# Expert layers: a gathered slot holds 32 tokens by four experts, and two slots are multiplied together in four sets of 32 columns

## The chip, the cores and the metric

One core of a Trainium2 chip runs the whole program. The metric is the device time of one execution in microseconds (us).

The engines are TensorE (PE in the profile; its weight loads are PEld), VectorE (DVE), ScalarE (ACT), GpSimd (POOL) and SyncE (SP). They run side by side, each through its own list in order, and wait for one another on semaphores. POOL issues the indirect transfers (gathers); SP issues the plain ones.

## The reference: what is computed

A decoder trunk of two layers for 512 prompt tokens and 8 sample tokens, all in float32, model width 1024. Layer 0 mixes tokens by a gated delta rule, layer 1 by latent attention with a paged cache. After each mixer comes the channel mixer, called PEER here, which is what the change is about:

```python
def peer_ffn(xn, w_q, sub_keys, u_tab, v_tab):
    q = (x2 @ w_q).reshape(T, PEER_HEADS, 2, PEER_HALF)
    s = jnp.einsum('thpd,hpnd->thpn', q, sub_keys)        # 2 x 128 keys per head
    ...                                                    # top 16 of each, then top 16 of the 256 sums
    h = jnp.einsum('td,ted->te', xb, u_tab[ib])            # per token, 8 heads x 16 experts
    act = jax.nn.gelu(h, approximate=False) * gb
    return jnp.einsum('te,ted->td', act, v_tab[ib])
```

So each token takes 128 expert rows out of a table of 16384, each row a u vector and a v vector of 1024 floats (8 KB together), a dot product with the token, a GELU and a gate, and the weighted sum of the v vectors. Each token has its own experts, so the rows are gathered one by one.

## The kernel before, in words

`peer` (L1429) runs once per layer. The prompt's 512 tokens are four tiles of 128. A **unit** is one head of one tile: 128 tokens by 16 experts, `UNITS` = 32 per layer. Units 0 to 15 take tiles 0 and 1 in turn, units 16 to 31 tiles 2 and 3 (`tile_of`, L1498). A unit is 16 **slots**; a slot is one gather of 128 rows of 8 KB (1.05 MB) into one of the 8 places of `ring` (L1455). So a layer has 512 slots, plus 8 for the sample tokens at its end. Before the change a slot holds 64 tokens by two experts: partition p of slot c holds an expert of token p mod 64.

The way of one slot, c of unit u:

- **POOL** (L1566) waits until the slot's place is free, which is the semaphore `pv` of the slot 8 places earlier, and issues the gather.
- **DVE** (L1761) waits for the landing and multiplies the u half by `rep`, the normed tokens repeated for the two experts, summing into one column of `hs`.
- **ACT** makes the GELU (L1642), multiplies by the gate (L1646) and writes the slot's entry of `diag` (L1650), a 128x64 matrix with the weights on two diagonals.
- **PE** (L1951) multiplies `diag` by the v half in two matmuls, one per half of the 1024 columns: each has 64 array columns and 512 moving columns, and they go to two halves of the partitions of a PSUM bank `acc`. Eight slots add up into one bank, and DVE adds the bank to `x` (`add`, L1721). The second matmul raises `pv` by one.

Between these, and in the same lists, stands the selection for the next unit: PE makes scores after the `pv` of slot 0 (`score`, L1895), DVE finds the top 16 in two parts after slots 1 and 4 (`retrieve`, L1705), PE spreads the 16 columns of indices over the two halves of the partitions after slot 5 (`lay`, L1905), DVE writes them as `idx` at slot 7 (`place`, L1710), and the same is done for the gates at slots 8 to 12. PE also projects the queries of the next head (L1883).

`rep` for a tile is made by `repeat` (PE, L1887) and `repeated` (ACT, L1606): a matmul with a constant that picks 64 tokens and writes them twice over the partitions, then a copy out of PSUM. It is done 4 times per tile: 2 groups of 64 tokens by 2 halves of the width. One PSUM bank (`pq`) serves, so each matmul waits for the copy before it. For tile 0 this is ahead of the first unit, between the scores and `lay` on PE; for tiles 1 and 3 in slots 0 to 3 of units 0 and 16; for tile 2 in slots 2 to 5 of unit 15.

Part of the latent attention is also run in these lists as a background (`Causal`, called as `back` at every slot number n from `BACK[layer]`, L1424): in layer 0 from unit 16 on, in layer 1 from unit 0 to about unit 14. It has transfers of its own on SP, and steps on PE, ACT and DVE with due slots.

Of the kernel before, what the change touches and what calls it, by code (L numbers as in the profile page):

```python
# [30 lines left out]
P = 128  # L31
D = 1024
# [29 lines left out]
N_CONST = C_REP + 2  # L62
HALF = D // 2
TG = 64
GS = SEQ // TG
# [770 lines left out]
class TopK:  # L836


    def __init__(self, core, ctx, n):
# [6 lines left out]
        self.crest = sb(ctx, "crest", [n, TOPK, TOPK])  # L846
# [77 lines left out]
class Causal:  # L924
# [369 lines left out]
    def tensor(self, pe, m):  # L1294
        s, core, at, bank = self.s, self.core, self.s.at, self.bank
        if m == 0:
            after(pe, *self.ready["banks"])
        if self.half == 0:
# [130 lines left out]
def peer(core, layer, oT, os, w_out, kept):  # L1429
# [6 lines left out]
    with Marks(core, "peer", **{f"o_w{k}": 16 for k in range(4)}, gain=32, inp=32, w0=32, w1=32, o_made=1, o_added=1, square=1, paired=1, mean=1,  # L1436
               root=1, inverse=1, row=1, turned=1, copied=1, copied2=1, q_first=4, first_out=4, q_made=2, q_out=2, scored=1, top=TOP_STEPS,
               exped=1, gate=2, mixed=2, placed=1, gated=1, rep_made=4, rep_out=4, dot=TOPK, gelu=TOPK, factor=TOPK, diag=TOPK, pv=TOPK, added=2,
# [15 lines left out]
        rep = core.sbuf(ctx, "rep", [P, 4, D])  # L1454
# [9 lines left out]
        diag = core.sbuf(ctx, "diag", [P, RING, TG])  # L1464
# [5 lines left out]
        spread = core.sbuf(ctx, "spread", [H * NS, 2, H, TOPK])  # L1470
# [3 lines left out]
        sac = core.sbuf(ctx, "sac", [P, NS, TG])  # L1474
# [13 lines left out]
            "xn": (at("rep_made", 3 - 2 * layer, 4),),  # L1488
            "x": (at("added", HEADS - 1, 2),),
            "banks": ((s["o_added"], done), (s["copied"], (done + 1) // 2), (s["copied2"], done // 2), (s["mean"], done), (s["first_out"], 4))})  # L1490
# [7 lines left out]
        def tile_of(u):  # L1498
            return 2 * (u // HEADS) + u % 2

# [22 lines left out]
        with nc.Block() as block:  # L1523
# [54 lines left out]
            def _(act):  # L1578
# [27 lines left out]
                def repeated(t, i):  # L1606
# [3 lines left out]
                    act.activation(rep[:, 2 * (t % 2) + i // 2, column(i % 2)], pq[:, :], ACT.Copy).then_inc(s["rep_out"], 1)  # L1610
# [16 lines left out]
                for i in range(4):  # L1627
                    repeated(0, i)
# [8 lines left out]
                for u in range(UNITS):  # L1637
                    a, hh = u % 2, u // 2 + 1
                    for c in range(TOPK):
# [10 lines left out]
                        act.activation(diag[:, c % RING, :], core.const[:, C_PAIR, 0:TG], ACT.Copy, scale=hgg[a][:, c:c + 1]).then_inc(s["diag"], 1)  # L1650
# [6 lines left out]
                        if u in (0, HEADS) and c < 4:  # L1657
                            repeated(tile_of(u + 1), c)
                        if u == HEADS - 1 and 2 <= c < 6:
                            repeated(2, c - 2)  # L1660
# [19 lines left out]
            def _(dve):  # L1680
# [12 lines left out]
                def row(g):  # L1693
                    after(dve, (s["inverse"], g + 1))
                    if 4 <= g < GS:
                        after(dve, at("rep_made", (g - 4) // 2, 4))
# [33 lines left out]
                dve.memset(sac[:, :, :], 0.0).then_inc(s["szero"], 1)  # L1730
# [21 lines left out]
                for u in range(UNITS):  # L1752
                    a = u % 2
                    for c in range(TOPK):
                        n = TOPK * u + c
                        if c == 0:
                            after(dve, at("rep_out", tile_of(u), 4))
# [3 lines left out]
                        dve.scalar_tensor_tensor(ring[:, c % RING, 0:D], ring[:, c % RING, 0:D], 1.0, rep[:, 2 * a + c // RING, :],  # L1761
# [26 lines left out]
                        if u == UNITS - 1:  # L1788
# [989 lines left out]
```

## Time and profile before

| | us |
|---|---|
| median of 3 runs | 3997.41 |
| lowest and highest | 3995.16, 4000.92 |
| span of the profiled execution, first to last instruction | 3986.4 |
| PE busy | 3005.8 |
| DVE busy | 2474.6 |
| ACT busy | 1535.0 |
| POOL busy | 1289.7 |

The trace is of one execution. No time of that execution from outside is given beside its span; the median stands 11.0 us above the span. In the span the gathers of layer 0 run from 695 to about 2120 us and those of layer 1 from 2515 to about 3965 us. A row that groups instructions gives the count, the busy time (overlaps counted once), the mean time of one in ns, then the idle time ahead of them and what ended it. A float32 matmul stands as two instructions, since it is done in two passes. PEclk is the granted clock, 1.00 being the full one.

### The profile page before, as it was taken

How to read it: one execution, taken by the hardware profiler on the slowest of the kernel's cores; microseconds unless marked ns; L12 is line 12 of the kernel's file. 1: busy time of each engine (PE TensorE's matmuls, PEld its weight loads, DVE VectorE, ACT ScalarE, POOL GpSimd, SP SyncE). 2: the span in 40 equal slices, each digit the busy share in tenths (PEclk: the TensorE clock that was granted, in tenths of full speed). 3: DMA queues.
4: the chain of work that ended last, by engine and by line, in shares of the span. 5: the costliest groups of instructions: out<-in, count | busy, mean ns of one | idle time of the engine just before them, and what ended most of it. 6: DMA issues, size and time to landing. Idle time of an engine off the chain costs nothing. (4 is left out here: it accounts for less than half of the span.)

```text
span 3986.4 us, 45941 instructions
## 1 busy us (share of the span) xinstructions
PE 3005.8 (75%) x14557; PEld 1439.4 (36%) x14557; DVE 2474.6 (62%) x6084; ACT 1535.0 (39%) x4402; POOL 1289.7 (32%) x1172
## 2 busy tenths in 40 slices
PE   7997888777666677768757798776777876666666
PEld 6886775322212122223313575322232222222221
DVE  2665443676676667767773343476677677667675
ACT  2352121444343344446432221344544444334332
POOL 0004330444434333333441110233334344334433
PEclk9998788988778788888878898888888988787778
DMA  2211002999999999999996453799999999999998
GB/s 89 73 51 55 13 13 71 404 420 416 420 414 418 405 397 387 411 366 384 402 421 244 165 204 144 291 375 390 381 375 415 405 404 421 413 420 413 411 421 334
DMA packets 234350, 1261.33 MB, mean 316 GB/s; under 512 B 32008, under 2 KB 71952, under 8 KB 97552
## 3 DMA queue, kind: packets, MB, share of 16 engines
q0 software_dynamic: 153600, 1133.58, 69.8%
q1 hardware_dynamic: 80528, 125.08, 9.1%
q8 instruction: 105, 1.72, 0.2%
q14 instruction: 117, 0.96, 0.1%
HBM read 1244.25 MB, written 14.19 MB: 316 GB/s over the span
## 5 line engine op out<-in xcount | busy, mean ns | idle before, releaser
L1951 PE MATMUL acc<-ring,diag 128*64 128x512 f32 x4096 | 1339.0, 751 | 751.3 <-ACT diag L1650 748.9
L1569 POOL DMA_INDIRECT ring<-in_uv,idx x1024 | 1119.1, 1093 | 1895.3 <-PE acc L1951 1635.2
L1761 DVE SCALAR_TENSOR_TENSOR ring<-ring,rep 128x1024 f32<-128x1024 f32 x1024 | 1230.6, 1221 | 368.9 <-DMA ring<-in_uv,idx 309.3
L1951 PEld LDWEIGHTS acc<-ring,diag 128*64 128x64 f32 x4096 | 250.3, 158 | 1494.2 <-ACT diag L1650 1317.8
L1642 ACT ACTIVATE hg<-hs 128x1 f32<-128x1 f32 x1024 | 203.7, 199 | 1141.1 <-DVE ring L1761 1139.1
L1650 ACT ACTIVATE diag<-const,hgg 128x64 f32<-128x64 f32 x1024 | 356.4, 348 | 33.4
L1646 ACT ACTIVATE hgg<-hg,weigh_by 128x1 f32<-128x1 f32 x1024 | 302.0, 295 | 33.2
L1883 PE MATMUL big<-xnT,w 128*128 128x264 f32 (+1 forms) x960 | 297.1, 435 | 0.0
L1883 PEld LDWEIGHTS big<-xnT,w 128*128 128x128 f32 x960 | 174.8, 203 | 185.0 <-issue 166.4
L298 PE MATMUL acc<-xnT,w 128*128 128x260 f32 x1024 | 230.2, 386 | 0.7 <-ACT inp L419 0.7
L298 PEld LDWEIGHTS acc<-xnT,w 128*128 128x128 f32 x1024 | 196.3, 192 | 38.4 <-issue 7.5
L1725 DVE TENSOR_TENSOR x<-acc,x 128x512 f32<-128x512 f32 x128 | 88.1, 688 | 117.2 <-PE acc L1951 117.2
L1642 ACT ACT_TABLE_LOAD x102 | 130.9, 1283 | 1.8
L875 DVE MAX8 sv<-mix 128x8 f32<-128x128 f32 x128 | 31.8, 290 | 150.5 <-PE mix L1902 150.3
L561 POOL TENSOR_TENSOR gU<-const,cols 128x512 f32<-128x512 f32 x8 | 8.4, 1045 | 340.8 <-POOLq L135 301.2
L1604 ACT ACTIVATE q<-big 128x264 f32<-128x264 f32 (+1 forms) x60 | 23.3, 388 | 239.5 <-PE big L1883 175.8
L1839 PE MATMUL big<-wo,oT 128*64 128x512 f32 x384 | 96.6, 640 | 19.0 <-DMA wo<-in_w_mla_out 10.8
L2584 DVE COPY cT<-b 128x512 f32<-128x512 f32 x64 | 44.2, 691 | 85.0 <-PE b L2406 84.9
L770 DVE TENSOR_TENSOR U<-pB,U 128x256 f32<-128x256 f32 x48 | 20.4, 425 | 121.6 <-PE pB L626 121.6
L2363 ACT ACTIVATE cT<-b 128x512 f32<-128x512 f32 x64 | 38.1, 596 | 145.1 <-PE b L2406 145.1
L1761 DVE DVE_READ_ACCUMULATOR ring<-ring,rep 128x1 f32 x1024 | 84.9, 83 | 0.0
L1614 ACT ACT_TABLE_LOAD x64 | 82.1, 1283 | 1.1
(571 smaller groups left out, 4057.7 us busy)
## 6 DMA issues: line engine op xcount, KB each, us to landing
w<-in_w_peer SPq DMA_DIRECT2D x64, 512.0 KB
w<-in_w_gdn SPq DMA_DIRECT2D x32, 512.0 KB, 3.6
ring<-in_uv,idx POOLq DMA_INDIRECT x1024, 12.3
wo<-in_w_mla_out SPq DMA_DIRECT2D x8, 1024.0 KB, 11.5
wo<-in_w_uq SPq DMA_DIRECT2D x8, 768.0 KB, 14.2
out_ssm_s<-states SPq DMA_DIRECT2D x4, 1024.0 KB, 5.1
wo<-in_w_gdn_out SPq DMA_DIRECT2D x4, 1024.0 KB, 8.2
sk<-in_keys SPq DMA_DIRECT2D x64, 64.0 KB
```

The lines of the kernel that those rows point to most:

```text
L298: last = pe.matmul(acc[c % 2][:, r, :], w[:, c, k, :], xnT[:, k, PART * r:PART * r + PART], start=k == 0, stop=k == KD - 1)
L1569: pool.indirect_dma_start(out=ring[:, c % RING, :], out_offset=None, in_=uv, in_offset=bass.IndirectOffsetOnAxis(ap=idx[u % 2][:, c:c + 1] ...
L1614: act.activation(k.e[:, :], k.tv[:, :], ACT.Exp, bias=k.low[:, 0:1], accum_out=k.z[:, 0:1]).then_inc(s["exped"], 1)
L1642: act.activation(hg[a][:, c:c + 1], hs[a][:, c:c + 1], ACT.Gelu).then_inc(s["gelu"], 1)
L1646: act.activation(hgg[a][:, c:c + 1], hg[a][:, c:c + 1], ACT.Copy, scale=weigh_by[a][:, c:c + 1]).then_inc(s["factor"], 1)
L1650: act.activation(diag[:, c % RING, :], core.const[:, C_PAIR, 0:TG], ACT.Copy, scale=hgg[a][:, c:c + 1]).then_inc(s["diag"], 1)
L1725: dve.tensor_tensor(core.x[:, g, :], acc[i][:, :], core.x[:, g, :], ALU.add).then_inc(s["added"], 1)
L1761: dve.scalar_tensor_tensor(ring[:, c % RING, 0:D], ring[:, c % RING, 0:D], 1.0, rep[:, 2 * a + c // RING, :], ALU.mult, ALU.mult, accum_ou ...
L1839: last = pe.matmul(summed(g)[rows(j), :], lhs, wo[:, kk, column(j)], start=kk == 0, stop=kk == KD - 1)
L1883: last = pe.matmul(pq[:, 0:n], w[:, p, kk, :], xnT[:, kk, 0:n], start=kk == 0, stop=kk == KD - 1)
L1951: last = pe.matmul(acc[i][rows(j), :], diag[:, r, :], ring[:, r, D + HALF * j:D + HALF * j + HALF], start=r == 0, stop=r == RING - 1)
L2584: dve.tensor_copy(cT[g % 2][:, 1, :, :], b1[g % 2][:, :, :]).then_inc(s["half1"], 1)
```

## The change

A slot now holds 32 tokens by four experts. Two slots, c - 1 and c, are multiplied together: four matmuls (two slots by two halves of the width), each with 32 array columns, each into its own 32 partitions of the bank. `diag` is 32 columns wide. PE waits for the `diag` of the odd slot only, and then raises `pv` twice.

```diff
-C_REP = C_PAIR + 1 ... N_CONST = C_REP + 2
+C_REP = C_PAIR + 1 ... C_QUAD = C_REP + 4; N_CONST = C_QUAD + 1; SUB = 32
-        rep = core.sbuf(ctx, "rep", [P, 4, D])
+        rep = core.sbuf(ctx, "rep", [P, 8, D])
-        diag = core.sbuf(ctx, "diag", [P, RING, TG])
+        diag = core.sbuf(ctx, "diag", [P, RING, SUB])
...
+        def repeat_bank(i):
+            return spare[:, :] if i % 2 else pq
+        def subs(i, b):
+            return slice(TG * i + SUB * b, TG * i + SUB * b + SUB)
...
# ACT
-                    act.activation(rep[:, 2 * (t % 2) + i // 2, column(i % 2)], pq[:, :], ACT.Copy).then_inc(s["rep_out"], 1)
+                    act.activation(rep[:, 4 * (t % 2) + i // 2, column(i % 2)], repeat_bank(i), ACT.Copy).then_inc(s["rep_out"], 1)
-                for i in range(4):
+                for i in range(8):
                     repeated(0, i)
-                        act.activation(diag[:, c % RING, :], core.const[:, C_PAIR, 0:TG], ACT.Copy, scale=...)
+                        act.activation(diag[:, c % RING, :], core.const[:, C_QUAD, 0:SUB], ACT.Copy, scale=...)
                         if u in (0, HEADS) and c < 4:
-                            repeated(tile_of(u + 1), c)
+                            for i in range(2 * c, 2 * c + 2):
+                                repeated(tile_of(u + 1), i)
...
# DVE
-                        ... rep[:, 2 * a + c // RING, :], ...
+                        ... rep[:, 4 * a + 2 * (c // RING) + c % 2, :], ...
-                dve.memset(sac[:, :, :], 0.0)        # ahead of the units
+                            if c == 0:               # in the last unit
+                                dve.memset(sac, 0.0)
...
# PE
 def repeat(t, i):
-                    g = 2 * t + i // 2
-                    after(pe, (s["row"], g + 1), at("rep_out", t, i))
+                    g = 2 * t + i // 4
+                    after(pe, (s["row"], g + 1), at("rep_out", t, i - 1))
...
-                    pe.matmul(pq[:, :], core.const[:, C_REP + i % 2, :], normed(g), ...)
+                    pe.matmul(repeat_bank(i), core.const[:, C_REP + i % 4, :], normed(g), ...)
 def lay(v, e, src):
                     for i in range(2):
-                        for r in range(2):
-                            last = pe.matmul(pR[rows(r), e, RING * i:RING * i + RING], core.const[:, C_ID, rows(i)], src[:, RING * r:RING * r + RING], ...)
+                        for b in range(2):
+                            for r in range(4):
+                                last = pe.matmul(pR[SUB * r:SUB * r + SUB, e, RING * i + b:RING * i + RING:2], core.const[:, C_ID, subs(i, b)], src[:, 4 * r:4 * r + 4], ...)
...
                         n, r, i = TOPK * u + c, c % RING, c // RING
-                        after(pe, at("diag", u, c + 1))
-                        if r == 0:
-                            after(pe, at("added", u - 1, i + 1) if u else (s["o_added"], 4))
-                        for j in range(2):
-                            last = pe.matmul(acc[i][rows(j), :], diag[:, r, :], ring[:, r, D + HALF * j:D + HALF * j + HALF], start=r == 0, stop=r == RING - 1)
-                        last.then_inc(s["pv"], 1)
+                        if c % 2:
+                            after(pe, at("diag", u, c + 1))
+                            if r == 1:
+                                after(pe, at("added", u - 1, i + 1) if u else (s["o_added"], 4))
+                            for b in range(2):
+                                for j in range(2):
+                                    last = pe.matmul(acc[i][subs(j, b), :], diag[:, r - 1 + b, :], ring[:, r - 1 + b, D + HALF * j:D + HALF * j + HALF],
+                                                     start=r == 1, stop=r == RING - 1)
+                                last.then_inc(s["pv"], 1)
...
-    nc = bacc.Bacc("TRN2", target_bir_lowering=False, num_devices=1)
+    nc = bacc.Bacc("TRN2", target_bir_lowering=False, num_devices=1, dynamic_dma_scratch_size=4096)
```

`rep` doubles to 32 KB of each partition, and the room comes from elsewhere: `crest` now lies in `rest`, `spread` and `sac` lie in `rep`, `diag` is half as wide, and the scratch area that the program sets aside for the descriptors of POOL's gathers is set to 4096 bytes per partition by name (it was the default). Waits on `rep_made` and `rep_out` count to 8, the background waits for the last copy out of `spare` ahead of its first step there, and `repeat` waits for `mean` where the bank `spare` is shared with the means.

## Rows read from the trace of the kernel before

**Rows 1.** The page's part 2: mean busy share of the DMA engines, 40 slices.

```profile
DMA  2211002999999999999996453799999999999998
```

**Rows 2.** Stretches of time: start:end, length, busy us by engine, PEclk, DMA share, GB/s.

```profile
760.00:1380.00 620.00, 429.54 (x1632) 137.98 (x1628) 433.92 (x1084) 258.09 (x817) 251.58 (x235) 0.82 1.01 417
1380.00:2000.00 620.00, 475.58 (x1798) 178.08 (x1798) 433.71 (x1141) 299.15 (x883) 232.84 (x214) 0.86 0.98 391
2000.00:2110.00 110.00, 69.52 (x228) 16.92 (x228) 80.94 (x200) 46.47 (x150) 45.11 (x44) 0.75 1.01 421
2560.00:3200.00 640.00, 484.71 (x1936) 182.90 (x1938) 440.53 (x1121) 294.51 (x848) 241.21 (x212) 0.86 0.99 388
3200.00:3940.00 740.00, 502.69 (x1799) 153.91 (x1800) 521.27 (x1315) 301.30 (x983) 308.00 (x287) 0.79 1.01 416
```

**Rows 3.** The same in pieces of 20 us: first and last under 0.97.

```profile
1400.00:1420.00 20.00, 15.73 (x50) 5.64 (x50) 13.04 (x36) 10.64 (x31) 5.89 (x5) 0.66 0.91 355
...
2900.00:2920.00 20.00, 17.03 (x64) 6.73 (x63) 16.36 (x39) 9.66 (x29) 6.62 (x6) 0.76 0.90 320
```

**Rows 4.** The page's part 5: costliest groups.

```profile
L1951 PE MATMUL acc<-ring,diag 128*64 128x512 f32 x4096 | 1339.0, 751 | 751.3 <-ACT diag L1650 748.9
L1569 POOL DMA_INDIRECT ring<-in_uv,idx x1024 | 1119.1, 1093 | 1895.3 <-PE acc L1951 1635.2
...
L1761 DVE SCALAR_TENSOR_TENSOR ring<-ring,rep 128x1024 f32<-128x1024 f32 x1024 | 1230.6, 1221 | 368.9 <-DMA ring<-in_uv,idx 309.3
```

**Rows 5.** The DMA view, 760:1380: gathers, median us from issue to landing.

```profile
ring<-in_uv,idx POOLq DMA_INDIRECT x235, 14.6
```

**Rows 6.** The DMA view, 1380:2000.

```profile
ring<-in_uv,idx POOLq DMA_INDIRECT x214, 10.2
```

**Rows 7.** PE in order of time, decode stage: one pass alone, then 32 columns wide.

```profile
2300.66 0.27 PE L2402 MATMUL b<-const,c 128*128 128x128 f32 x1
2300.77 0.38 PE L2406 MATMUL b<-const,kr 128*128 128x128 f32 x2
2301.08 0.65 PE L2413 MATMUL pL<-cT,ql 128*32 128x128 f32 x16
2301.54 0.40 PE L2415 MATMUL pL<-rT,qr 128*32 128x128 f32 x8
```

**Rows 8.** Waits in 2560:3200: who waited for whom; us, times, longest.

```profile
POOL ring L1569 <- PE acc L1951: 388.0, 180, 15.7
...
DVE sv L875 <- PE mix L1902: 40.2, 11, 8.0
```

**Rows 9.** PE in order of time, in layer 1's background.

```profile
2858.63 1.08 PE L1951 MATMUL acc<-ring,diag 128*64 128x512 f32 x4
...
2861.34 1.08 PE L1951 MATMUL acc<-ring,diag 128*64 128x512 f32 x4
...
2886.77 1.98 PE L1951 MATMUL acc<-ring,diag 128*64 128x512 f32 x4 [3.26 <-ACT diag L1650]
2888.67 1.23 PE L1902 MATMUL mix<-sk,q 128*128 128x128 f32 x4
```

**Rows 10.** DVE in order of time, the same place.

```profile
2889.94 0.50 DVE L875 MAX8 sv<-mix 128x8 f32<-128x128 f32 x2 [7.97 <-PE mix L1902]
```

**Rows 11.** PE and POOL in order of time, the start of layer 1's gathers.

```profile
2507.09 1.13 PE L1893 MATMUL big<-xn,const 128*128 128x512 f32 x2
...
2512.74 1.10 PE L1893 MATMUL big<-xn,const 128*128 128x512 f32 x2 [0.78 <-ACT rep L1610]
...
2513.77 0.41 PE L1910 MATMUL mix<-index,const 128*64 128x8 f32 x8
...
2514.67 0.94 POOL L1569 DMA_INDIRECT ring<-in_uv,idx  x1 [98.32 <-DVE idx L1713]
```

**Rows 12.** Groups of POOL's gathers with rows of 16 KB and of 1 KB.

```profile
L2322 POOL DMA_INDIRECT c<-in_cache_latent,idx x16 | 15.0, 938 | 59.3 <-PE pMO L2458 56.2 <-issue 3.0
L2322 POOL DMA_INDIRECT ks<-in_cache_kscale,idx x8 | 7.6, 951 | 50.1 <-DVE m L2545 49.5 <-issue 0.6
```

More of the change, by code:

```diff
@@ L1297, in tensor @@
             after(pe, *self.ready["banks"])
+        if m == (15, 6)[self.half]:
+            after(pe, *self.ready["spare"])
         if self.half == 0:
@@ L1788, in _ @@
                         if u == UNITS - 1:
+                            if c == 0:
+                                dve.memset(sac, 0.0).then_inc(s["szero"], 1)
                             if c == 1:
@@ L1855, in turn @@
                     if g == 3:
-                        after(pe, at("rep_out", 0, 4))
+                        after(pe, at("rep_out", 0, 8))
                     if g == 4:
@@ L1876, in queries @@
                         if hh == 1:
-                            after(pe, at("rep_out", 1, 4))
+                            after(pe, at("rep_out", 1, 8))
                         if hh == H:
@@ L1880, in queries @@
                         if hh == H + 1:
-                            after(pe, at("rep_out", 3, 4))
+                            after(pe, at("rep_out", 3, 8))
                     for kk in range(k0, k1):
@@ L1887, in repeat @@
                 def repeat(t, i):
-                    g = 2 * t + i // 2
-                    after(pe, (s["row"], g + 1), at("rep_out", t, i))
-                    if t == 2:
-                        after(pe, at("q_out", H - 1, 2))
-                    pe.matmul(pq[:, :], core.const[:, C_REP + i % 2, :], normed(g), start=True, stop=True).then_inc(s["rep_made"], 1)
+                    g = 2 * t + i // 4
+                    after(pe, (s["row"], g + 1), at("rep_out", t, i - 1))
+                    if t == 0 and i == 1:
+                        after(pe, (s["mean"], 2))
+                    if t == 1 and i == 0:
+                        after(pe, (s["mean"], 4))
+                    if t == 2 and i == 0:
+                        after(pe, at("q_out", H - 1, 2), (s["mean"], GROUPS))
+                    pe.matmul(repeat_bank(i), core.const[:, C_REP + i % 4, :], normed(g), start=True, stop=True).then_inc(s["rep_made"], 1)
                 def score(v):
@@ L1908, in lay @@
                     for i in range(2):
-                        for r in range(2):
-                            last = pe.matmul(pR[rows(r), e, RING * i:RING * i + RING], core.const[:, C_ID, rows(i)], src[:, RING * r:RING * r + RING], start=True, stop=True)
+                        for b in range(2):
+                            for r in range(4):
+                                last = pe.matmul(pR[SUB * r:SUB * r + SUB, e, RING * i + b:RING * i + RING:2], core.const[:, C_ID, subs(i, b)],
+                                                 src[:, 4 * r:4 * r + 4], start=True, stop=True)
                     last.then_inc(s["mixed"], 1)
@@ L1931, in _ @@
                 project((2, 3), 6, KD)
-                for i in range(4):
+                for i in range(8):
                     repeat(0, i)
@@ L1935, in _ @@
                 lay(0, 0, index)
+                after(pe, at("rep_out", 0, 8))
                 pair(2, 2)
@@ L1964, in _ @@
                         if u in (0, HEADS) and c < 4:
-                            repeat(tile_of(u + 1), c)
+                            for i in range(2 * c, 2 * c + 2):
+                                repeat(tile_of(u + 1), i)
                         if u == HEADS - 1 and 2 <= c < 6:
-                            repeat(2, c - 2)
+                            for i in range(2 * c - 4, 2 * c - 2):
+                                repeat(2, i)
                         if u >= HEADS and a == 0 and c == SAMPLE_C:
@@ L2714, in host @@
     tiles += [(i // (2 << l) == j // (2 << l)) & ((i >> l) % 2 == 1) & ((j >> l) % 2 == 0) for l in range(LEVELS)]
-    tiles += [i % TG == j % TG] + [j == TG * e + i % TG for e in range(2)]
+    tiles += [i % TG == j % TG] + [j == TG * e + SUB * b + i % SUB for b in range(2) for e in range(2)] + [i % SUB == j % SUB]
     rows = np.zeros((GROUPS * TG, D), np.float32)
```

27 lines of the change are left out of this document (15 added, 12 removed).

## The prediction

> **What bounds the kernel now.** Read the slices of the DMA engines first [rows 1]. Two long blocks stand at 9: the gathers of layer 0 and of layer 1, about 1425 and 1450 us of the 3986.4 us span. The rest has no expert slots and the change doesn't touch it.
>
> Next, the stretches [rows 2]. Without a background (760 to 1380, 2000 to 2110, 3200 to 3940) the DMA share is 1.01 at 416 to 421 GB/s. With it (1380 to 2000 and 2560 to 3200) it is 0.98 and 0.99 at 391 and 388 GB/s. The rate falls by 7 to 8%, the share only by 2 to 3%: most of the lost rate is the background's own small packets, which keep the engines busy at fewer bytes, and no faster PE gives that back. What can be given back is idle DMA time: (1.01 - 0.98) x 620 = 18.6 us and (1.01 - 0.99) x 640 = 12.8 us, 31 us in all. Cut into pieces of 20 us, each background has eight pieces under 0.97 (the first and the last of the 16 in [rows 3]); all pieces of the two summed against 1.01 give 36 us, and 3 us more stand in layer 1's quiet stretch. I take 36 us as the headroom.
>
> Then the groups [rows 4]. PE's acc line is busy 1339.0 us, POOL waits 1635.2 us for it, and DVE waits 309.3 us for the gathers. POOL's wait looks like the bound and is not: a gather takes 14.6 us from issue to landing in the quiet stretch [rows 5], and at one gather of 1.05 MB per 2.49 us (421 GB/s) that is 5.9 gathers in the queue. With the background it is 10.2 us [rows 6], 4.1 gathers. This reserve is what the change works on, from both sides.
>
> **PE's part.** A slot now costs four passes of 512 columns, two side by side: the list moves on by 1.03 us for a lone matmul of two passes of that width (2512.74 to 2513.77, [rows 11]), and the slot shows as 1.08 us at the full clock and 1.98 at the low one [rows 9]. After, two slots are eight passes, four side by side. The trace has that form: 16 passes of 128 columns in 32 array columns take 2301.54 - 2301.08 = 0.46 us, 0.115 per four, where one pass alone takes 2300.77 - 2300.66 = 0.11 [rows 7]. So four cost 1.05 times one, and two slots 2 x 0.515 x 1.05 = 1.08 us instead of about 2.1. Bounds: 1.03 (perfect) and 2.1 (no more overlap than now). I take 1.08. The acc line falls from 1339.0 to about 670 us.
>
> The Trainium skill ("TensorE: Matmul & The Clock Gate", section "Measured speedup vs the span model") gives 2.38 times for three column tiles of 512, 0.79 per tile. By that a pair would be an estimate of 8 x 0.515 / (4 x 0.79) = 1.30 us. The trace's 0.95 per tile disagrees for short passes; the sum would be the same, because PE is not the last wait in most units.
>
> `lay` goes from 8 passes to 32, twice per unit. 8 take 0.41 us with their tail [rows 11], 0.05 each; at that rate 32 take 1.6 us, at the 0.029 of [rows 7] 0.93. So +0.5 to +1.2 us, I take +0.9, 1.8 per unit, against 16 x 0.5 = 8 us saved on PE. `repeat` adds 16 matmuls per layer of 1.03 us, 17 us on PE, and ACT 16 copies; both have room in 69 to 77% and 42 to 48% busy shares [rows 2].
>
> The clock takes some back. The granted clock goes with PE's busy share: 0.86 at 77%, 0.82 at 69%, 0.75 at 63% [rows 2]. In the two backgrounds PE is busy 960 us [rows 2], of which 426 gathers (POOL's counts, 214 + 212) x 1339.0 / 1024 = 557 are acc [rows 4]. Without half of that PE will be near 60 to 65%, so a clock near 0.77. The other 403 us then take 0.86 / 0.77 = 1.12 times as long, +48 us, against 278 saved. PE is still freer by about 170 us of 1260 with `lay` counted.
>
> **What it is worth.** In the quiet stretches nothing: the queue is never empty. In the backgrounds it shortens two things. First, parts where PE sets the pace: from 2858.63 to 2861.34 one slot takes 2.71 us with no idle time on PE [rows 9], over the 2.49 of a gather. Second, the scores. Now PE makes them behind the `pv` of slot 0, which waits for that slot's `diag`; at 2886.77 it had waited 3.26 us, the scores came at 2888.67, and DVE, idle 7.97 us, only then went on [rows 9, 10]. After, slot 0 has no multiplication, so the scores follow slot 15 at once. DVE waited 40.2 us for scores in 2560:3200, 11 times [rows 8]. Bounds: nothing (the queue empties for other causes, such as weights that PE waits for) to all 36 us. I take 60%, -22 us, as both causes named stand at places where the DMA share is low.
>
> **Pairing.** The even slot is free only with the odd one: it is asked for again later by one dot product, 1.22 us [rows 4], where DVE is behind, or one gather, 2.49 us, where it is not. Where the queue keeps gathers this costs nothing. Behind the waiting PE stand the background's matmuls, but they now run before the wait of an even slot rather than behind it. Where the queue runs empty, at some 16 places, half find an even slot held: 16 x 0.5 x 1.22 = 10 us. Bounds: 0, and one such place per unit and more (27 background units, 426 gathers / 16): 27 x 1.6 x 0.5 x 1.85 = 40. I take +8, as after a stall PE catches up at DVE's 1.22 us per slot, not at its own 1.98.
>
> **The start of each layer.** `lay` for the first gather stands behind `repeat` on PE. The four begin at 2507.09 and `lay` at 2513.77, paced by the one bank; the first gather goes out at 2514.67 [rows 11]. With two banks eight take 8 x 1.03 = 8.2 us: `lay` at 2515.3, +1.5, and it lasts longer itself, +0.5 to +1.2. The first gather is 2.3 us later, in a stage that from there is bound by the transfers, so all of it counts. The ninth gather waits for slots 0 and 1 and two more ACT copies each, about +0.7 net. 3 us per layer, +6; bounds +2 and +10. The memset that moves into the last unit, the narrower `diag`, the moved buffers and the waits that count to 8: nothing, hidden under the transfers. The end of the layers: its last gathers queue behind full ones, nothing.
>
> **Sum.** -22 + 8 + 6 = -8 us: a span of 3978.4, and with the 11.0 us by which the median stands over the span, 3989. The measurement can tell about 0.2%, 8 us, from no change, so this lies on that edge. The likeliest case alone: 3981 to 3997.
>
> **Rivals.**
> - *All the idle DMA time goes.* For it: PE 77% busy and both causes above. Against: waits for the background's own transfers stay. -36 + 6 = -30: 3967.
> - *Nothing is given back, since the gathers hide it anyway.* For it: DMA share 0.98 and 0.99. Then 0 + 6: 4003; with some pairing cost, up to 4008.
> - *The held even slot starves the queue in the backgrounds.* The reserve there is 4.1 gathers at the median against stalls like DVE's 7.97 us; with half a gather less it empties more often. For it: PE's relief comes only after a stall, the loss at it. Against: 10.2 us of reserve. It decides where more than one place per unit runs empty. +40 - 16 + 6 = +30: 4027.
> - *It doesn't do what it says, or the smaller scratch area limits the gathers in flight.* If four sets don't run together, a pair keeps its 2.1 us and holds slots longer: about +30. POOL's 938 ns for rows of 16 KB and 951 for 1 KB [rows 12] speak for one entry per row, so that 8 gathers of 128 rows stay few. If only about two gathers fitted, every unit's stall of about 7 us would outlast 5 us of reserve: 64 x 2, +130. I put 4027 and more on both.
>
> The Trainium skill ("DMA: Bandwidth & Descriptors", section "Terms") has descriptors of 16 bytes in rings in SBUF. By that, 4096 bytes are an estimate of 256 per ring, and 8 gathers of 128 rows over 16 engines want 64; no run here shows the count.
>
> **Chances.** Forecast 0.33, all idle time gone 0.18, nothing back 0.26, pairing starves 0.17, the last 0.06. Faster by over 0.2%: 0.18 + 0.24 of cases around the forecast's edge and beyond = 0.42. Within 0.2%: 0.31. Slower: 0.17 + 0.06 + a few hundredths of the third = 0.27. The range 3958 to 4030 holds the first four but for their tails.
>
> **What would show it.** acc busy near 670 us and a pair's eight passes in about 1.1 us (2.1: wrong). Clock below 0.80 in the backgrounds. DMA share there 1.00 and above (0.96: the pairing starves). DVE's waits for scores nearly gone. First gather of each layer 2 to 3 us later behind its scores. Landing at most one gather shorter in the quiet stretches. The prediction is wrong if the DMA share stays and the time moves, or if the backgrounds' rate passes 400 GB/s.

## The result and the profile after

| | before | after |
|---|---|---|
| median | 3996.28 us (3992.54 to 4000.92, 4 runs) | 3965.91 us (3959.23 to 3968.22, 4 runs) |
| span of the profiled execution | 3986.4 | 3963.0 |
| granted clock, mean | 0.849 | 0.757 |

The ratio is 0.9925, 95% interval 0.9907 to 0.9942: 30 us faster, where 8 were forecast. The time is inside the range of 3958 to 4030, which reaches from faster to slower; it is outside the 3981 to 3997 of the forecast's own case, and it is the first rival's number (3967).

The two spans differ by 23 us only. In every other profiled execution here the time is 2.0 to 2.2 us over the span, so the profiled execution of before took about 3988.5 us, less than each of the four above: it was a quick one.

The costliest groups of the kernel after, columns as in [rows 4]:

```profile
L1580 POOL DMA_INDIRECT ring<-in_uv,idx x1024 | 1149.7, 1123 | 1837.0 <-PE acc L1974 1458.4
L1773 DVE SCALAR_TENSOR_TENSOR ring<-ring,rep 128x1024 f32<-128x1024 f32 x1024 | 1238.1, 1222 | 501.1 <-DMA ring<-in_uv,idx 423.4
L1974 PE MATMUL acc<-ring,diag 128*32 128x512 f32 x4096 | 783.9, 852 | 1111.6 <-ACT diag L1661 1111.3
```

PE's line fell by 555 us; the time fell by 30. DVE now waits 423.4 us for the gathers against 309.3: a larger part of the run is bound by the transfers alone, and there less work on PE gives nothing.

The stretches, columns as in [rows 2], 10 us earlier than there in layer 0 and 20 in layer 1, which starts earlier now:

```profile
750.00:1370.00 620.00, 338.78 (x2342) 118.92 (x2342) 436.00 (x1098) 249.91 (x811) 263.18 (x234) 0.66 1.01 415
1370.00:1990.00 620.00, 391.65 (x2498) 169.53 (x2498) 451.70 (x1177) 308.46 (x922) 246.52 (x222) 0.75 1.01 408
2540.00:3180.00 640.00, 401.70 (x2610) 167.22 (x2610) 451.63 (x1144) 296.48 (x868) 242.76 (x218) 0.77 0.99 397
3180.00:3920.00 740.00, 370.51 (x2608) 128.69 (x2609) 518.03 (x1299) 298.93 (x982) 322.97 (x284) 0.63 1.01 415
```

Both backgrounds carry more (391 and 388 GB/s before). Layer 0's is as full as a quiet stretch now; layer 1's share stays at 0.99. Fixed stretches hold a little more or less of a layer each time. A cleaner ruler is the work itself: the time between POOL's issues of the layer's first gather, its 257th and its 513th. The table is worked out from these starts in each profiled execution:

| us | L0 quiet | L0 background | L1 background | L1 quiet |
|---|---|---|---|---|
| before | 675.3 | 730.2 | 760.5 | 660.4 |
| after | 677.7 | 705.2 | 746.2 | 663.5 |
| difference | +2.4 | -25.0 | -14.3 | +3.1 |

So the backgrounds gave 39.3 us and the quiet stretches cost 5.5. The balance, 33.8 us, is more than the 23 us between the spans, since the time ahead of the first gather and between the layers was 11 us longer in this execution of after. How far to trust one execution: number 4 below is before but for its scratch area and has 674.9, 733.5, 761.9 and 660.9 us, so up to 0.5 us off in the quiet stages and 3.3 in the backgrounds. The 2 to 3 us in the quiet stages are small, but all kernels made from after by one small edit (numbers 9, 11 and 12 below) have them: 676.4 to 677.4 and 662.8 to 664.2 us.

The background stages by themselves, layer 0 and layer 1, before and then after:

```profile
1370.70:2100.90 730.20, 542.11 (x2026) 194.15 (x2026) 513.76 (x1339) 345.31 (x1032) 277.20 (x256) 0.84 0.99 396
2514.67:3275.20 760.53, 565.37 (x2244) 215.49 (x2244) 521.99 (x1332) 347.62 (x1008) 291.26 (x257) 0.87 0.99 391
```

```profile
1379.40:2084.60 705.20, 426.26 (x2742) 177.85 (x2742) 516.45 (x1340) 342.07 (x1033) 286.03 (x256) 0.73 1.01 409
2503.43:3249.60 746.17, 468.15 (x3060) 198.12 (x3060) 524.95 (x1332) 348.00 (x1016) 285.04 (x256) 0.77 0.98 397
```

In layer 0 the share rises. In layer 1 it doesn't, and the stage is 14 us shorter all the same: the time that the DMA engines were busy fell from 751 to 735 us each (721 to 713 in layer 0; number 4 below has 747 and 722), with the bytes the same to 0.3%. What is still idle there stands behind two waits of PE, 19.50 and 14.95 us, for weights of the background's own. The second, with POOL's next gather behind it and the stretch around it:

```profile
2737.13 1.65 PE L1398 MATMUL spare<-wo,xn 128*128 128x384 f32 x2 [14.95 <-DMA wo<-in_w_uq]
```

```profile
2741.34 0.94 POOL L1580 DMA_INDIRECT ring<-in_uv,idx  x1 [18.17 <-PE acc L1974]
```

```profile
2730.00:2750.00 20.00, 12.87 (x89) 6.82 (x89) 10.30 (x27) 11.20 (x25) 6.28 (x6) 0.75 0.62 237
```

PE cannot free a slot while it stands in that wait. In 20 us at each of the two places (shares 0.66 and 0.62) 15 us of DMA time are idle. Before, PE waited 11.30 and 11.61 us there: it went on 53.5 and 232.0 us after the layer's first gather then and goes on 55.4 and 233.7 us after it now, so a PE that is ahead only waits longer.

DVE's waits for the scores in 1370:1990 and 2540:3180 of after (us, times, longest); before they were 50.6 us in 14 waits in 1380:2000, and 40.2 in 11 [rows 8]:

```profile
DVE sv L877 <- PE mix L1920: 9.4, 3, 7.4
...
DVE sv L877 <- PE mix L1920: 13.4, 6, 5.7
```

And how it looks at the head of a unit. PE in order of time: the pair (14, 15) waits for its `diag`, the scores follow at once. The second fence is DVE, which has other work and takes them without a wait, where it sat idle for 7.97 us in [rows 10]:

```profile
2903.52 1.63 PE L1974 MATMUL acc<-ring,diag 128*32 128x512 f32 x8 [4.54 <-ACT diag L1661]
2905.08 1.23 PE L1920 MATMUL mix<-sk,q 128*128 128x128 f32 x4
```

```profile
2906.55 1.21 DVE L1773 SCALAR_TENSOR_TENSOR ring<-ring,rep 128x1024 f32<-128x1024 f32 x1
2907.69 0.08 DVE L1773 DVE_READ_ACCUMULATOR ring<-ring,rep 128x1 f32 x1
2907.69 0.48 DVE L877 MAX8 sv<-mix 128x8 f32<-128x128 f32 x2
```

The start of layer 1 after, PE and then POOL, as in [rows 11]:

```profile
2494.94 1.12 PE L1911 MATMUL big<-xn,const 128*128 128x512 f32 x2
...
2501.52 1.02 PE L1911 MATMUL spare<-xn,const 128*128 128x512 f32 x2
2502.48 0.43 PE L1929 MATMUL mix<-index,const 128*32 128x4 f32 x32
```

```profile
2503.43 0.94 POOL L1580 DMA_INDIRECT ring<-in_uv,idx  x1 [99.22 <-DVE idx L1726]
```

Eight repeats take 2502.48 - 2494.94 = 7.54 us against 2513.77 - 2507.09 = 6.68 for four: the second bank hides ACT's copies. `lay` with 32 passes takes 0.43 us against 0.41 with 8.

### The profile page after: what moved, and what is told of

It reads as the page before. It is cut to its first block and busy times, and to the rows that moved or that the text cites. A ratio compares the mean times of both kernels' runs of the same rounds, so it can differ in the third digit from the quotient of the medians.

```text
span 3963.0 us, 52296 instructions
## 1 busy us (share of the span) xinstructions
PE 2580.9 (65%) x17693; PEld 1369.3 (35%) x17693; DVE 2479.9 (63%) x6084; ACT 1532.5 (39%) x4434; POOL 1321.3 (33%) x1172
## 5 line engine op out<-in xcount | busy, mean ns | idle before, releaser
L1580 POOL DMA_INDIRECT ring<-in_uv,idx x1024 | 1149.7, 1123 | 1837.0 <-PE acc L1974 1458.4
L1773 DVE SCALAR_TENSOR_TENSOR ring<-ring,rep 128x1024 f32<-128x1024 f32 x1024 | 1238.1, 1222 | 501.1 <-DMA ring<-in_uv,idx 423.4
L1974 PE MATMUL acc<-ring,diag 128*32 128x512 f32 x4096 | 783.9, 852 | 1111.6 <-ACT diag L1661 1111.3
L1974 PEld LDWEIGHTS acc<-ring,diag 128*32 128x32 f32 x4096 | 95.9, 126 | 1498.8 <-ACT diag L1661 1455.4
L1661 ACT ACTIVATE diag<-const,hgg 128x32 f32<-128x32 f32 x1024 | 329.3, 322 | 33.4
L1897 PE MATMUL big<-xnT,w 128*128 128x264 f32 (+1 forms) x960 | 312.5, 464 | 3.1 <-ACT rep L1621 3.1
L1897 PEld LDWEIGHTS big<-xnT,w 128*128 128x128 f32 x960 | 198.4, 224 | 152.1 <-issue 122.8
L1738 DVE TENSOR_TENSOR x<-acc,x 128x512 f32<-128x512 f32 x128 | 88.1, 688 | 88.4 <-PE acc L1974 88.4
L2427 PE MATMUL b<-const,c 128*128 128x128 f32 x256 | 66.3, 296 | 15.0 <-DMA c<-in_cache_latent,idx 15.0
L1920 PEld LDWEIGHTS mix<-sk,q 128*128 128x128 f32 x256 | 50.6, 273 | 72.6 <-issue 70.7
## 6 DMA issues: line engine op xcount, KB each, us to landing
wo<-in_w_mla_out SPq DMA_DIRECT2D x8, 1024.0 KB, 11.6
```

The lines of the kernel that those rows point to most:

```text
L1580: pool.indirect_dma_start(out=ring[:, c % RING, :], out_offset=None, in_=uv, in_offset=bass.IndirectOffsetOnAxis(ap=idx[u % 2][:, c:c + 1] ...
L1661: act.activation(diag[:, c % RING, :], core.const[:, C_QUAD, 0:SUB], ACT.Copy, scale=hgg[a][:, c:c + 1]).then_inc(s["diag"], 1)
L1738: dve.tensor_tensor(core.x[:, g, :], acc[i][:, :], core.x[:, g, :], ALU.add).then_inc(s["added"], 1)
L1897: last = pe.matmul(pq[:, 0:n], w[:, p, kk, :], xnT[:, kk, 0:n], start=kk == 0, stop=kk == KD - 1)
L1974: last = pe.matmul(acc[i][subs(j, b), :], diag[:, r - 1 + b, :], ring[:, r - 1 + b, D + HALF * j:D + HALF * j + HALF], start=r == 1, stop= ...
L2427: pe.transpose(b0[g % 2][:, j, :], c[a][:, BQ * g + j, 0:P], core.ident)
```

## The experiments

Ratios are to the kernel before, five rounds each, with the 95% interval. Stage times are read as in the table above, each from one execution.

**1. The scores alone.** In PE's list the scores of the next unit go ahead of slot 0's wait; nothing else is changed.

```diff
+                        if u < UNITS - 1 and c == 0:
+                            score(u + 1)
                         after(pe, at("diag", u, c + 1))
...
-                            if c == 0:
-                                score(u + 1)
```

> The kernel before, with one edit: PE makes the scores of the next unit ahead of slot 0's wait instead of behind its multiplication. Theory S (the gain came from the scores no longer standing behind slot 0's diag): ratio to before 0.994 to 0.996, DVE's wait for scores in the backgrounds (50.6 + 40.2 us) falls under 25 us, rates there near 400 GB/s. Theory P (the gain came from PE needing half the time for acc): ratio 0.998 to 1.000, the waits fall as well but the rates in the backgrounds stay within 4 GB/s of 391 and 388.

0.9944 [0.9932, 0.9957], 3969.6 us. The backgrounds take 720.6 and 752.1 us (-9.6, -8.4), the quiet stages 674.9 and 659.5. A line moved by one place gives three quarters of the gain, with acc at 1327.1 us. Theory S has the ratio, though not the whole of its signs: DVE's waits for the scores only fell to 36.0 us (9) and 24.0 (9). The longest, 19.65 us, stands behind a wait of PE of 9.69 us for the background's weights, after which PE had its late slots to do first.

**2. PE's relief alone.** Same order as before, half of the moving columns.

```diff
-                            last = pe.matmul(acc[i][rows(j), :], diag[:, r, :], ring[:, r, D + HALF * j:D + HALF * j + HALF], start=r == 0, stop=r == RING - 1)
+                            last = pe.matmul(acc[i][rows(j), 0:HALF // 2], diag[:, r, :], ring[:, r, D + HALF * j:D + HALF * j + HALF // 2], start=r == 0, stop=r == RING - 1)
```

> The kernel before with acc matmuls of 256 moving columns instead of 512: half of the weighted v sum is left out. PE's time for a slot falls by half with no pairing, no new layout and the scores where they were. Theory P: ratio 0.990 to 0.994, both backgrounds above 400 GB/s. Theory S: 0.997 to 1.000.

0.993 [0.9917, 0.9943], 3964.3 us, clock 0.748, acc 915.0 us. Backgrounds 715.7 and 739.7 us (-14.5, -20.8) at 403 and 401 GB/s, as theory P had it.

**3. Pairing alone.** Slots multiplied in pairs, with 64 array columns and at PE's old price; the scores stand at slot 0, where nothing is waited for now, so it is to be held against number 1.

```diff
...
+                        if c % 2:
+                            after(pe, at("diag", u, c + 1))
...
+                            for b in range(2):
+                                for j in range(2):
+                                    last = pe.matmul(acc[i][rows(j), :], diag[:, r - 1 + b, :], ring[:, r - 1 + b, D + HALF * j:D + HALF * j + HALF],
+                                                     start=r == 1 and b == 0, stop=r == RING - 1 and b == 1)
+                                last.then_inc(s["pv"], 1)
```

> The kernel before with PE multiplying slots c-1 and c together at the odd c, still 64 array columns each, so PE's time stays and the even slot is held; the scores come at slot 0 without a wait, as in the changed kernel. If pairing has a price of its own (my 8 us, bounds 0 to 40) and the scores' place is worth little: ratio 1.001 to 1.005. Theory S: 0.995 to 0.998. The slower rival, pairing starves the queue: above 1.006.

0.9967 [0.9954, 0.998], 3979.5 us. Against number 1 that is +0.0023 (+-0.0018 from the two intervals), +9 us: 679.2 and 662.0 us in the quiet stages (+4.3, +2.5), 760.3 in L1's background (+8.2), 710.0 in L0's (-10.6). The wait that grew most in 760:1380 had 12.2 us (13 times) in number 1 and 11.9 in before:

```profile
DVE idx L1713 <- PE mix L1910: 34.1, 15, 2.8
```

It is DVE's wait for `lay`, which PE has behind the pair (4, 5). The lists of rows come later, with DVE's dot products behind them. Its wait for the scores grew too, from 3.5 to 10.5 us.

**4. The scratch area alone.**

```diff
-    nc = bacc.Bacc("TRN2", target_bir_lowering=False, num_devices=1)
+    nc = bacc.Bacc("TRN2", target_bir_lowering=False, num_devices=1, dynamic_dma_scratch_size=4096)
```

> The kernel before with the scratch area for the gathers' descriptors at 4096 bytes per partition, nothing else. If one entry per row holds: ratio 0.999 to 1.001 and landing medians of 14.6 and 10.2 us as before. If the area limits the gathers in flight: landing medians shorter by several us and a ratio above 1.005.

1.0007 [0.9998, 1.0017], landing medians of 14.0 and 10.1 us. It does nothing here.

**5. The kernel after without the relief.** Each multiplication of a pair is done twice.

```diff
-                            for b in range(2):
+                            for b in range(4):
                                 for j in range(2):
-                                    last = pe.matmul(acc[i][subs(j, b), :], diag[:, r - 1 + b, :], ring[:, r - 1 + b, D + HALF * j:D + HALF * j + HALF],
+                                    last = pe.matmul(acc[i][subs(j, b % 2), :], diag[:, r - 1 + b % 2, :], ring[:, r - 1 + b % 2, D + HALF * j:D + HALF * j + HALF],
...
-                                last.then_inc(s["pv"], 1)
+                                if b > 1:
+                                    last.then_inc(s["pv"], 1)
```

> The changed kernel with every acc matmul done twice (the expert output is doubled): the time that the four sets save is spent again, all else as changed. If the relief of PE adds to the scores' place: ratio to before 0.995 to 0.998, near the 0.9967 of pairing with the scores ahead. If the scores' place alone made the gain (theory S): 0.992 to 0.994, as the changed kernel.

1.0076 [1.0059, 1.0093], 4017.9 us. Its acc line:

```profile
L1974 PE MATMUL acc<-ring,diag 128*32 128x512 f32 x8192 | 1244.9, 736 | 846.8 <-ACT diag L1661 846.5
```

With PE's old load the change is 30 us slower than before by the ratio, 60 slower than itself; neither range of the expectation had that. Every stage but L0's background lost: 690.6, 712.8, 770.4, 669.3 us. DVE's wait for `lay` in 760:1340 is the 34 us of number 3 again:

```profile
DVE idx L1726 <- PE mix L1929: 37.8, 14, 3.2
```

It is 43 us worse than number 3 at the same acc time to 1%. Several things differ: the even slot comes free after three quarters of the pair's time, in number 3 after half; the repeats and ACT's copies are doubled; `lay` has 32 passes. What each costs was not taken apart.

**6. The scores behind the first pair**, in the kernel after.

```diff
-                            if c == 0:
+                            if c == 1:
                                 score(u + 1)
```

> The changed kernel with the scores of the next unit behind the pair of slots 0 and 1, where they wait for slot 1's diag. Theory S: 0.997 to 1.000. Theory P: 0.992 to 0.995. Both acting on one limited idle time: 0.994 to 0.997, with DVE's waits for scores in the backgrounds above 60 us.

1.0262 [1.0243, 1.0282], 4093.4 us, outside all three ranges, the quiet stages 712.0 and 701.2 us. DVE's waits in 760:1340; in the kernel after this is 1.9 us in 2 waits:

```profile
DVE sv L877 <- PE mix L1920: 54.1, 14, 4.1
```

The quiet stages lose 34.3 and 37.7 us with 16 units each: 2.1 to 2.4 us per unit, one slot's time. The landing there is 10.8 us and the DMA share 0.98: a quiet stretch is not out of reach of PE's order.

**7. The same in the kernel before:** the scores behind slot 1's multiplication instead of slot 0's.

```diff
-                            if c == 0:
+                            if c == 1:
                                 score(u + 1)
```

> The kernel before with the scores of the next unit behind slot 1's multiplication instead of slot 0's. In the kernel after the scores behind the pair (0, 1) gave 1.0262 against 0.9925, some 2 us for each of 62 units. Theory (the sensitivity belongs to the order of PE's list and VectorE's wait for the scores, whether slots are paired or not): 1.010 to 1.03, and waits of VectorE for the scores in nearly every unit of the quiet stretches, which have 1.9 us of them in all now. Rival (only the pairing makes it so, since the pair is complete later): 1.000 to 1.005.

1.0145 [1.0121, 1.0168], 4046.7 us: 15.5 and 7.9 us in the quiet stages, 10.8 and 16.1 in the backgrounds. In 760:1380:

```profile
DVE sv L875 <- PE mix L1902: 52.6, 15, 4.7
```

The 1.9 us that the expectation gives for these waits are those of the kernel after; in before they are 10.0 us, 9 times. So the sensitivity belongs to the chain scores, retrieval, rows of the next unit, with paired slots or single ones. From slot 0's wait it costs 53 us to go one slot later (medians of the same rounds) and gives 22 to go one earlier. Number 6 went the whole way, from ahead of any wait to behind slot 1's: that step is 0.0201 in before (number 7 less number 1), 80 us, and 0.0337 in after, 135 us by the ratios. That pairing makes it dearer is likely, and was not tested alone.

**8. The kernel after, not paired.** Array sets of 32 columns, but each slot's two are multiplied as soon as its `diag` is there, two side by side; the scores ahead.

```diff
-                        if c % 2:
-                            after(pe, at("diag", u, c + 1))
...
+                        after(pe, at("diag", u, c + 1))
...
+                        for j in range(2):
+                            last = pe.matmul(acc[i][subs(j, r % 2), :], diag[:, r, :], ring[:, r, D + HALF * j:D + HALF * j + HALF],
+                                             start=r < 2, stop=r >= RING - 2)
+                        last.then_inc(s["pv"], 1)
```

> The changed kernel, but each slot's two matmuls of 32 columns go as soon as its own diag is there: no even slot is held, and two sets side by side instead of four unless PE is behind. The price of holding was measured at about 0.0023 of the time (pairing with scores ahead 0.9967 against scores ahead alone 0.9944). If that price is also in the changed kernel: 0.989 to 0.9915. If PE's relief is what counts and is lost with the pairing: 0.993 to 0.996.

0.9958 [0.9942, 0.9974], 3977.0 us, acc 1270.3 us, clock 0.848. The median is 11 us above after's and near number 1's; the intervals touch, so that relief outweighs the wait for the odd slot is likely from this pair alone, not more.

**9. The first list of rows earlier:** `lay` for unit 0 after five of the eight repeats.

```diff
-                for i in range(8):
+                for i in range(5):
                     repeat(0, i)
                 after(pe, at("top", 0, TOP_STEPS))
                 lay(0, 0, index)
+                for i in range(5, 8):
+                    repeat(0, i)
```

> The changed kernel with lay of the first unit's indices after five of the eight repeats instead of after all. The first gather of each layer comes 12.7 us after the scores in the changed kernel; here 10.5 to 11 us, so the time falls by 2 to 4 us and the ratio to before is 0.9915 to 0.992. If the first gather does not set the layer's end: no change, 0.9925.

0.9929 [0.9912, 0.9946], 3960.2 us. The first gather goes out 10.7 us behind the scores instead of 12.7, but no difference from after can be measured; 4 us are under what the intervals tell.

**10. Numbers 1 and 2 together,** in the kernel before.

> The kernel before with the scores of the next unit made ahead of slot 0's wait, and with 256 instead of 512 moving columns in each multiplication of diag (half of the weighted sum of the v vectors is left out). Alone the first edit gave 0.9944 and the second 0.993. Theory (both work on the same limited idle DMA time of the backgrounds): 0.991 to 0.993, hardly better than the second alone, backgrounds' share 1.00 to 1.01, quiet stretches unchanged. Rival (two causes that add up): 0.9874, between 0.986 and 0.989, which needs a rate in the backgrounds above 410 GB/s in both layers.

0.9902 [0.9883, 0.9921], 3951.6 us: between the two. Simply added they would give 0.9874, the better alone is 0.993. Its stretches 1380:2000 and 2560:3200:

```profile
1380.00:2000.00 620.00, 419.43 (x1854) 197.95 (x1854) 456.10 (x1186) 311.08 (x918) 244.43 (x223) 0.74 1.01 407
2560.00:3200.00 640.00, 430.40 (x2016) 205.54 (x2014) 469.64 (x1189) 310.54 (x899) 258.84 (x227) 0.77 1.00 406
```

In layer 1's background nothing adds up (740.2 us, 739.7 with the relief alone); in layer 0's some does (709.7 against 715.7). So the causes are two, and part of what they give is the same. Neither theory's range held the value, and the interval reaches into both.

**11. A long piece on DVE one slot later,** in the kernel after.

```diff
-                            if c == 4:
+                            if c == 5:
                                 retrieve(u + 1, 1)
```

> The kernel after with the second part of the retrieval on VectorE (6.5 us in one piece) after slot 5 instead of slot 4, so that the pair (4, 5) is complete before the long piece and the even slot 4 is not held across it. Theory A (the price of pairing lies in even slots that are held while VectorE does a long piece): 0.9885 to 0.9915, the quiet stretches 2 us shorter each. Theory B (the price is spread over all pairs, or lies at the other long pieces): 0.992 to 0.993, as the kernel after. Rival: the scores' results or the list of rows for the next unit are late by one slot, so 0.994 to 0.998.

0.9956 [0.9941, 0.9971], 3973.7 us: slower than after, as the expectation's last rival had it. The quiet stages didn't move (677.4, 664.1), so no price of pairing was found at this place. DVE's additions wait longer for acc, since PE stands in `lay`'s wait with the pair (6, 7) behind it; after has 88.4 us here:

```profile
L1738 DVE TENSOR_TENSOR x<-acc,x 128x512 f32<-128x512 f32 x128 | 88.0, 688 | 118.8 <-PE acc L1974 118.7
```

**12. These additions later,** in the kernel after.

```diff
-                        if c == 9:
+                        if c == 11:
                             add(u, 0)
-                        if c == 2 and u:
+                        if c == 3 and u:
```

> The kernel after with its two additions of a unit's result on VectorE later: acc 0 after slot 11 instead of 9, acc 1 after slot 3 instead of 2 of the next unit. In the kernel after VectorE waits 88.4 us for acc in these additions, 51.1 us of it in 30 of the pieces of the two quiet stretches (14 waits in 760:1380, 16 in 3200:3900), 19.6 us in 2560:3200. Expected wait after the edit: under 20 us. Theory A (these waits delay dot products at places where the queue is short, so they are part of what pairing costs): 0.989 to 0.991, each quiet stretch and the second background 1 to 3 us shorter. Theory B (they stand where VectorE has time before the next landing, so they only move its idle time to the wait for the gather): 0.992 to 0.993 as the kernel after, with VectorE's wait for the gathers longer by about what the other wait loses.

0.9934 [0.992, 0.9948], 3967.9 us: as after. The wait is gone and stands at the gathers instead, 485.5 us for 423.4:

```profile
L1773 DVE SCALAR_TENSOR_TENSOR ring<-ring,rep 128x1024 f32<-128x1024 f32 x1024 | 1237.0, 1222 | 561.6 <-DMA ring<-in_uv,idx 485.5 <-issue 73.0
L1738 DVE TENSOR_TENSOR x<-acc,x 128x512 f32<-128x512 f32 x128 | 87.7, 685 | 0.4 <-PE acc L1974 0.4
```

So 88 us of waits were worth nothing. In 760:1380 of after they are 25.0 us, and without them the quiet stage takes 676.4 us for 677.7; number 6's 54 us of another wait cost 34 us in the same stage. The wait for the scores has the rows of the next unit behind it, the wait for acc only an addition and dot products whose landing wasn't there yet. No kernel that does the whole work was measurably faster than after.

## Why the prediction came out as it did

The runs give the sum again, each term against its neighbour (1 us is 0.00025); the start is read from the trace alone:

| term | forecast | measured | from |
|---|---|---|---|
| scores ahead | in the -22 | -22 | number 1: -0.0056 |
| PE's relief, scores being ahead | in the -22 | -17 | number 10 less number 1: -0.0042 (+-0.0023) |
| pairing | +8 | +9 | number 3 less number 1: +0.0023 (+-0.0018) |
| start of the layers | +6 | +2 | first gather behind the first scores |
| scratch area | 0 | 0 | number 4 |
| sum | -8 | -28 | the change: -30 |

That the terms add up is no proof of each. The relief is worth 17 us where slots are single (number 10) and 60 where it is taken out of the kernel after (number 5): terms measured in one order don't hold in another.

**The step that failed is "I take 60%, -22 us"** for what the backgrounds give back: they gave 39. The forecast named two causes and priced them as one; either alone gives 18 to 35 us in the backgrounds.

**The headroom was right in layer 0 only.** The forecast was to fill idle DMA time. In layer 0 it does: 730.2 us at a share of 0.988 (to three places), filled to the measured 1.011, is 714 us, so 17 of the 25 us are idle time, and the other 8 are packets that took less time. In layer 1 the share stands at 0.99 before and 0.98 after, and the 14 us are all of the second kind, which the forecast had at nothing ("no faster PE gives that back"). Why the same bytes keep the engines busy for less time is open. So that 39 us came out beside the 36 counted as idle is in part luck. The forecast's own test, "wrong if the DMA share stays and the time moves", comes true in layer 1.

**The discount had a row.** Its reason, "weights that PE waits for", stood in the trace of before: 11.3 and 11.6 us in layer 1's background, 8.7 in layer 0's. In after they are 19.5, 14.9 and 12.8, and 15 us of layer 1's idle time stand behind the first two. The cause was right; 40% of everything was not how it acts. It took nothing in layer 0, where the share is 0.99 around that wait, and in layer 1 it took about as much as filling the other gaps gave, in the one execution of each that was read.

**The packets.** That most of the lost rate is the background's own small packets was partly right: 408 and 397 GB/s still stand under 415, in layer 0 with no idle time left. But "wrong if the rate passes 400" was set against the forecast's own rows: 391 x 1.01 / 0.98 is 403. Measured, 408 in layer 0 passes it. The test should have been worked out from the share.

**PE's part.** A pair takes 1.06 us at the full clock, 1.08 forecast, and two slots took 2.16 [rows 9]; this trace's own 32-column row was the right guide. By the ratio for three tiles that the Trainium skill gives ("TensorE: Matmul & The Clock Gate", "Measured speedup vs the span model") it would have been an estimate of 1.30, and the measurement decides against it here. The line fell to 783.9 and not to 670, since the clock went lower than the 0.77 that the forecast priced only for the backgrounds: 0.66 and 0.63 in the quiet stretches, where acc is most of PE's work. A pair at the lower of the two levels is nearly twice as long; 263 of the 512 pairs took over 1.85 us, 219 under 1.15. In 750:1370 the long ones are 69 of 116, in 1370:1990 they are 41 of 111. PE had been idle for 3.5 us ahead of a long pair on average, for 0.7 ahead of a short one:

```profile
2881.32 1.94 PE L1974 MATMUL acc<-ring,diag 128*32 128x512 f32 x8 [5.19 <-ACT diag L1661]
...
2886.91 1.07 PE L1974 MATMUL acc<-ring,diag 128*32 128x512 f32 x8 [0.41 <-ACT diag L1661]
```

These two stand in layer 1's background: the first after 5.19 us of idle time, the second 5.6 us later. The 0.75 and 0.77 in the backgrounds are what was forecast.

**Quiet stretches "nothing".** Wrong in sign and small: +5.5 us together. The landing fell from 14.6 [rows 5] to 13.1 us, by less than one gather as forecast; at which moments the cost arises was not read. Two edits can have a hand in it: pairing, since number 3 has +4.3 and +2.5 us over number 1 with the old repeats, and the doubled repeats, since number 8 takes 677.3 and 661.4 us with single slots. In layer 1's quiet stage number 2 takes 662.6 us and number 10 665.6 with neither, so layer 1's +3.1 can't be put down to one of the two.

**Pairing +8** was the right size from the wrong place. It was put at empty queues of the backgrounds; it was measured in the quiet stages and in layer 1's background, with `lay` behind a later pair as the wait that grew most (34.1 us against 12.2 in the quiet stage; 17.0 in the kernel after). Numbers 11 and 12 looked for its place at two points of DVE's list and found it at neither, so where exactly the 9 us lie is open, and so is the sign in layer 0's background, where number 3 was faster than number 1.

**The start, +6.** The first gather goes out 12.7 us behind the layer's first scores, 11.8 before: +0.9 per layer, not 2.3. Of that the repeats have 0.86 (7.54 - 6.68); the forecast took 8 x 1.03, but the two banks run at 0.94. `lay` has 0.02 and not 0.9: 32 passes of 4 columns took 0.43 us, 0.013 each, where the bounds had 0.05 from 8 passes with their tail and 0.029 from passes of 128 columns. The ninth gather's +0.7 was not seen: it goes out 18.5 us after the first before, 18.6 and 18.7 after. That the median stands 11.0 us over the span was counted as fixed; some 2.1 are, the rest was that one execution. The forecast of 3989 doesn't depend on it.

**The rivals.** "All the idle DMA time goes" had the right number, and the right reason in layer 0; in layer 1 the idle time stayed. "Nothing is given back" falls with numbers 1 and 2. "The held even slot starves the queue" is no empty threat: it is number 5, +30 us from this very kernel once PE's relief is taken out, though what of the 30 us is the held slot's was not taken apart. The smaller scratch area is number 4, nothing; the estimate from the Trainium skill ("DMA: Bandwidth & Descriptors", "Terms") had said the same, though no run shows the count of entries.

## What to carry to other kernels

When the transfers are the bound in most of a run, look for the stretches where their share falls, and for the waits there that hold up the next addresses or the next free slot. The place of such a wait in another engine's list counts for more than that engine's busy time: here the scores one slot later cost 53 us, one slot earlier gave 22, while 88 us of another wait gave nothing. Idle DMA time is a guide to what can be won and no sum: see what stands ahead of each gap, since a wait for a transfer stays where it is when the engine gets there sooner. A change that bundles an order with a faster form should be priced as two, each alone: moving the scores alone brings three quarters of what the whole change does.

## What the runs showed of the hardware

Four sets of 32 array columns run together in full for float32: a pair's eight passes of 512 columns take 1.06 us where four passes in two sets took 1.08. 32 passes of 4 columns in four sets took 0.43 us, 8 passes of 8 columns in two sets 0.41.

The clock took back a part of the relief: with half the moving columns acc fell to 915.0 us and with four sets to 783.9, at mean clocks of 0.748 and 0.757 against 0.849. 263 of the 512 pairs ran at the lower level, after 3.5 us of idle time on average. What this cost in time was not taken apart; with it the run was 30 us faster.

The same bytes can take the DMA engines different times: layer 1's background kept them busy for 751 us before and 735 after, with 297.1 and 296.3 MB. So share times length is not a fixed amount of work.
